# Moving an expert block's input load from GpSimd to ScalarE, in four transfers beside the result store

## What is computed

```python
def expert_block(args):                      # xb: 128 rows here; the kernel's blocks have 32
    xb, e = args
    hg, hu = jnp.split(xb @ w_gu[e], 2, axis=-1)
    return (jax.nn.silu(hg) * hu) @ w_down[e]
```

## Time and profile before

| | us |
|---|---|
| median of 3 runs (3356.11 to 3363.2) | 3362.7 |
| the profiled execution, as timed | 3372.45 |
| its span in the trace | 3370.8 |
| TensorE busy with matmuls in it | 2548.6 |
| VectorE busy | 1044.1 |
| ScalarE busy | 526.3 |
| GpSimd busy | 370.4 |

### The profile page before, as it was taken

The page is one execution under the profiler, slowest core; times in us unless marked ns, Lnnn a source line. Parts: engine busy times, 40 slices in busy tenths (PEclk is TensorE's granted clock), DMA queues, the critical chain, the costliest instruction groups (busy, mean ns, idle before and its releaser), DMA issues. The chain is left out here.

```text
span 3370.8 us, 75892 instructions
## 1 busy us (share of the span) xinstructions
PE 2548.6 (76%) x31542; PEld 1819.0 (54%) x31543; DVE 1044.1 (31%) x2767; ACT 526.3 (16%) x1257; POOL 370.4 (11%) x527
## 2 busy tenths in 40 slices
PE   8987958775998758775652897999999757667752
PEld 3456546554446446553442345989998335445531
DVE  0225322214107522211114303655653631111214
ACT  1034101101105101000001102422432000000100
POOL 0000111002000020000002001211210220000002
PEclk9988969988999869987775998987988678798976
DMA  5212059996110059999996000000000348999995
GB/s 203 81 45 113 17 194 353 366 353 225 66 75 26 15 213 366 371 375 397 391 390 242 29 25 0 1 0 0 0 0 1 134 180 318 389 380 384 367 391 194
DMA packets 110774, 646.52 MB, mean 192 GB/s; under 512 B 38290, under 2 KB 60050, under 8 KB 76900
## 3 DMA queue, kind: packets, MB, share of 16 engines
q1 hardware_dynamic: 41440, 567.30, 44.0%
q0 software_dynamic: 32896, 55.23, 5.0%
q10 hardware_dynamic: 36356, 22.86, 2.4%
HBM read 599.98 MB, written 45.09 MB: 191 GB/s over the span
## 5 line engine op out<-in xcount | busy, mean ns | idle before, releaser
L1162 PE MATMUL ps<-ring,arena 128*32 128x128 f32 x13440 | 460.1, 301 | 243.2 <-DMA ring<-in_experts 127.5
L1162 PEld LDWEIGHTS ps<-ring,arena 128*32 128x32 f32 x13440 | 422.2, 122 | 298.0 <-issue 150.0
L1171 PE MATMUL ps<-ring,arena 128*32 128x256 f32 x3360 | 263.9, 453 | 120.9 <-DMA ring<-in_experts 77.2
L1222 DVE TENSOR_TENSOR arena<-arena,ps 128x64 f32<-128x64 f32 x296 | 65.7, 222 | 713.3 <-ACT arena L1200 713.3
L1200 ACT ACTIVATE arena<-ps 128x64 f32<-128x64 f32 x296 | 66.1, 223 | 1304.3 <-PE ps L1162 1044.7
L1162 PE MATMUL ps<-arena 128*32 128x128 f32 x5504 | 189.1, 300 | 73.8 <-DMA arena<-in_experts 57.6
L1137 POOL DMA_DIRECT2D arena<-xybuf x148 | 100.3, 678 | 1277.1 <-DVE arena L1210 1235.6
L1171 PEld LDWEIGHTS ps<-ring,arena 128*32 128x32 f32 x3360 | 114.5, 126 | 231.6 <-DMA ring<-in_experts 90.8
L1162 PEld LDWEIGHTS ps<-arena 128*32 128x32 f32 x5504 | 171.6, 121 | 100.5 <-DMA arena<-in_experts 69.9
L1232 DVE COPY arena<-ps 128x256 f32<-128x256 f32 x148 | 62.9, 425 | 418.3 <-PE ps L1171 243.6
L355 PE MATMUL ps<-ring,arena 128*128 128x512 f32 x384 | 166.0, 593 | 3.1 <-PEq L192 3.1
(11 more groups left out here) (385 smaller groups left out, 3834.1 us busy)
## 6 DMA issues: line engine op xcount, KB each, us to landing
ring<-in_experts SPq DMA_DIRECT2D x165, 2048.0 KB, 38.1
arena<-in_experts SPq DMA_DIRECT2D x50, 2048.0 KB, 35.6
xt_mem<-in_experts SPq DMA_DIRECT2D x25, 2048.0 KB, 42.8
ring<-in_mixer_chunks SPq DMA_DIRECT2D x24, 2048.0 KB, 12.6
xybuf<-arena ACTq DMA_DIRECT2D x640, 32.0 KB, 11.6
arena<-xybuf POOLq DMA_DIRECT2D x160, 128.0 KB, 12.2
xybuf<-arena SPq DMA_DIRECT2D x1, 9216.0 KB, 25.6
rows<-in_ln_g POOLq DMA_DIRECT2D x6, 512.0 KB, 5.1
```

Of the source, the lines that this page charges most:

```text
L1162: ins = pe.matmul(ps[at, 2 + half, 0:P], xg[:, k, :], w_gu[half][:, k, q, :], start=(k == 0), stop=(k == NK - 1))
L1171: ins = pe.matmul(ps[at, 4, 0:W], hT[:, f, :], w_d[:, f, q * W:(q + 1) * W], start=(f == 0), stop=(f == NT - 1))
L1222: dve.tensor_tensor(hidden[:, half, :], silu_g[:, half, :], ps[:, 2 + half, HALF:P], ALU.mult)\
```

## The change

POOL only scatters. ScalarE issues the block loads, each as four transfers of 32 rows of 256 columns, two of them behind each pair of stores. It waits for the scatters, loads the first three blocks, and in block g loads block g + 3, into the buffer that block g - 1 had. Each block's four loads count up `s_loaded` by 64 instead of 16.

```diff
@@ POOL
                     for j in range(NT):
                         for n in range(2):
                             pool.indirect_dma_start(...).then_inc(s_sent, 16)
-                    pool.wait_ge(s_sent, 2 * NT * 16)
-                    fours = value(pool, slice(E + 2, E + 3), high=MAXB // AHEAD)
-                    for b in range(AHEAD):
-                        pool.dma_start(x_in[:, b, :], rows_at(b)).then_inc(s_loaded[b], 16)
-                    with pool.Fori(0, fours) as p:
-                        for b in range(AHEAD):
-                            g = AHEAD * p + b
-                            pool.wait_ge(s_xg, g + 1)
-                            pool.dma_start(x_in[:, b, :], rows_at(g + AHEAD)).then_inc(s_loaded[b], 16)
...
@@ ScalarE
+                    def rows_of_block(start, q):
+                        return xybuf[bass.ds(start, BLK), q * W:(q + 1) * W]
...
+                    def load_quarters(start, b, two):
+                        for q in two:
+                            act.dma_start(x_in[quarters[q], b, :], rows_of_block(start, q)).then_inc(s_loaded[b], 16)
...
                     fours = value(act, slice(E + 2, E + 3), high=MAXB // AHEAD)
+                    act.wait_ge(s_sent, 2 * NT * 16)
+                    for b in range(AHEAD - 1):
+                        load_quarters((b + 1) * BLK, b, range(4))
                     with act.Fori(0, fours) as p:
...
                             act.wait_ge(s_y, g + 1)
                             for half in range(2):
                                 store_quarters(g * BLK, freed, (2 * half, 2 * half + 1))
+                                load_quarters((g + AHEAD) * BLK, freed, (2 * half, 2 * half + 1))
                                 act.wait_ge(s_gu[half], g + 1)
                                 act.activation(silu_g[:, half, :], ...).then_inc(s_silu[half], 1)
...
@@ VectorE
-                            dve.wait_ge(s_loaded[after], p * 16 + 16 + 16 * (b == AHEAD - 1))
+                            dve.wait_ge(s_loaded[after], p * 64 + 64 + 64 * (b == AHEAD - 1))
```

More of the change, by code:

```diff
@@ L1089, in value @@
                 return eng.value_load(table[0:1, n], min_val=low, max_val=high)
-            def rows_at(g):
-                return xybuf[bass.ds((g + 1) * BLK, BLK), :].rearrange("r (q n) -> q r n", q=4)
             with nc.Block() as block:
@@ L1128, in _ @@
                                                     in_=x_tok[:, j, :], in_offset=None).then_inc(s_sent, 16)
-                    pool.wait_ge(s_sent, 2 * NT * 16)
-                    fours = value(pool, slice(E + 2, E + 3), high=MAXB // AHEAD)
-                    for b in range(AHEAD):
-                        pool.dma_start(x_in[:, b, :], rows_at(b)).then_inc(s_loaded[b], 16)
-                    with pool.Fori(0, fours) as p:
-                        for b in range(AHEAD):
-                            g = AHEAD * p + b
-                            pool.wait_ge(s_xg, g + 1)
-                            pool.dma_start(x_in[:, b, :], rows_at(g + AHEAD)).then_inc(s_loaded[b], 16)
-                    for b in range(AHEAD):
-                        pool.wait_ge(s_loaded[b], fours * 16 + 16)
                 @block.tensor
@@ L1182, in _ @@
                 def _(act):
+                    def rows_of_block(start, q):
+                        return xybuf[bass.ds(start, BLK), q * W:(q + 1) * W]
                     def store_quarters(start, b, two):
                         for q in two:
-                            act.dma_start(xybuf[bass.ds(start, BLK), q * W:(q + 1) * W], y_sb[quarters[q], b, :])\
-                               .then_inc(s_stored[b], 16)
+                            act.dma_start(rows_of_block(start, q), y_sb[quarters[q], b, :]).then_inc(s_stored[b], 16)
+                    def load_quarters(start, b, two):
+                        for q in two:
+                            act.dma_start(x_in[quarters[q], b, :], rows_of_block(start, q)).then_inc(s_loaded[b], 16)
                     for b in range(AHEAD - 1):
@@ L1204, in _ @@
                         act.wait_ge(s_stored[b], fours * 64 + 64)
+                    for b in range(AHEAD - 1):
+                        act.wait_ge(s_loaded[b], fours * 64 + 64)
                     act.activation(spot, eps_ln, ACT.Copy)
@@ L1213, in _ @@
                     dve.memset(spot, 0.0).then_inc(s_y, 1)
-                    dve.wait_ge(s_loaded[0], 16)
+                    dve.wait_ge(s_loaded[0], 64)
                     take_inputs(0)
```

## The result

| | before | after |
|---|---|---|
| median of 7 runs | 3363.2 us | 3391.3 us (3381.15 to 3404.6) |
| ratio | | 1.0086, 95% interval 1.0064 to 1.0108 |
| span of the profiled execution | 3370.8 us | 3392.1 us |

The change makes the kernel slower by 28 us, where 144 were forecast. The way was right. The forecast's own range, 3420 to 3600, missed it; the wider range of 3385 to 3640 holds it at its lower edge. The size was wrong by a factor of five.

What follows compares the result with a forecast made beforehand. The prediction took q10, ScalarE's queue, to bound dense stretches by its turns, one packet per weight packet, and weights to bound others. Its terms 43 + 45 + 20 + 17 + 19 = 144 us on 3362.7 gave 3507 us, range 3385 to 3640.

Steps and rivals of the forecast that it cites:

- a turn becomes shorter by 5%: Queues while weights stream: without q0's packets, turns go from 23.05 to 24.2 per us.
- rival B: Expert stages: stores' turns come 5% sooner and loads land faster, so 37 waiting copies save 15 us; 3348 us, chance 0.05.
- The shared queue: Expert stages: loads join stores on q10, 380 turns or 15.7 us a block while weights stream; terms +43, +45, +20, +17.
- my 43: First expert stage: q10 cannot follow, costing +3.3 us for each of 13 experts loaded during the stage.
- the 45 + 20: Second and third expert stages: +45 for pauses of q1 at 5.9 us each, +20 for TensorE's lag at their ends.
- The 17 for TensorE after a wait: Expert stages: slower matmuls after waiting, some 12 pauses, half of them long enough, at 2.9 us: +17 us.
- ScalarE's issuing: Expert blocks: load issues ahead of each Silu delay a block by 0.5 us, uncovered in 38 blocks: +19 us.
- The signs: Profile after: blocks about 16 us apart in stretches, dips of q1, transposes waiting for loads, loads landing in 25 to 35 us.
- The opening: Kernel start: ScalarE waits for the scatter and issues 12 loads before its table load and first Silu; cost 0.
- A: Queue q10: it takes more than a packet in a turn, or loads hide; only issuing costs, +19: 3382 us, chance 0.11.
- C: Expert stages: reserves don't help, each expert of more than one block waits for q10; 3685 us, chance 0.13.
- D: Whole kernel: nothing moves, since waits for weights cover all; 3363 us, chance 0.03.

Runs made afterwards that it cites:

- e6: As e2, but each load cut in two (eight loads of 32 rows of 512 bytes a block); 3459.55 us, 1.0267 of the kernel before.
- e10: The kernel before, POOL still loading, but in four transfers of 32 rows of 1 KB a block instead of one; 3276.41 us, ratio 0.9723.
- e2: As e1, but block g loads block g + 4 into its own buffer, a block deeper; 3334.89 us, 0.9898 of the kernel before.
- e1: The changed kernel with a block's four loads moved behind its second Silu; 3350.96 us, 0.9943 of the kernel before.
- e12: The kernel before with POOL's load as two transfers of 64 partitions instead of one; 3405.35 us, ratio 1.0104.
- e8: As e2, but the four stores too stand behind the second Silu; 3352.35 us, 0.9961 of the kernel before.
- e7: The kernel before plus a ScalarE Silu of constants behind each pair of stores, its end not waited for; 3369.03 us, ratio 1.0002.

## Why the prediction was right about the way and wrong about the size

*What bound the kernel.* Right: one packet for one packet, seen again in the changed kernel (1617 to 1616) and in e6 (2488 to 2487).

*"With q0's 5.0% out of 101.5% of the engines' time, a turn becomes shorter by 5%: 24.2 per us."* This step failed. It took the price of q0's load to be the load's own packets. In the same dense stretch 26.8 turns per us were measured (632 to 662 us), since the weights' own packets became faster: 0.570 us on average in place of 0.632. The row that could have warned was at hand: the earlier trace rows give 0.584 with few q0 packets, and 26.4 turns per us, which the forecast did not use. e10 gives the whole worth of this: the same loads by POOL without the spread shape are 2.8% faster, 93 us. The change gets that gain too: q1's packets took 1394 us in it and 1388 in e10, against 1483. My sum had no such term, and rival B, the only one with a gain, had 15 us for it.

*The shared queue.* Terms of 43 + 45 + 20 + 17 = 125 us. Between e10 and e2 the loads go from q0 to q10, with ScalarE's issues hidden: 1.75%, 59 us (in e2 they also leave later, behind the second Silu, and have 192 packets a block in place of 128; no run parts these). The smaller depth is another 15 (e2 to e1). So 74 us, in place of 125. The mechanism was as told: dips of q1 in stage one, and in the full stretches of stages two and three a block every 14 us in place of my 15.7, with 16.0 us of weights in place of 17.8. But the loss sat elsewhere. From e10 to e1 stage one grew by 305.6 - 283.5 = 22 us, half of my 43: its blocks were not 16 us apart for long, since q1 ran dry again and again and q10 drained. Stages two and three grew by 39 and 34, about the 45 + 20 that I had for both and more. That they stand at only 5 and 0 us against the kernel before is the weights' gain of 37 and 39 us in the same stages. (The three growths are 95 us together, where the whole kernel grew by 73: the stretch between stages two and three, which no change touches, took 1008.9 us in e10 and 993.4 in e1, and something between 993 and 1010 in the other runs.) The 17 for TensorE after a wait no run shows apart: its gate and up matmuls became dearer by 22 us in the three windows (649 to 671), but its whole busy time fell from 2548.6 to 2526.5 us.

*ScalarE's issuing.* Forecast +0.5 us a quiet block, 19 us; measured 1.06 us and 48 us (e1 against the change). I took 0.80 us for a pair of loads, less the 0.35 that ScalarE had to spare; but the pair costs 0.84 and 0.16 to 0.18 ahead of it, and the stores' pair went from 0.80 to 0.84, in both halves of the block, and so the second Silu is late by 1.06 and not by 0.45. And the cover that I counted on, the 8.3 us of the dense stretches, was itself removed: there most blocks take 6.5 to 9 us now, so the chain shows.

Together, relative to the kernel before: -93 + 59 + 15 + 48 = 29 us. That this meets the 28 measured is no proof: the four are the steps of one path, before to e10 to e2 to e1 to the change, and add up to the difference whatever their causes are. What they show is the size of each step at one corner of the square: along its other side, place is 31 and depth 32 us. My own terms came to 144, and the same parts measured 122; the missing -93 makes most of the error of 116. That 144 was near 122 is partly luck, since the queue's terms were 51 too large and ScalarE's 29 too small.

*The signs.* Dips of q1, waits for loads in place of waits for stores, one to one in full stretches and, there, loads landing in 25 to 35 us (33.4 from 1600 to 1660) came. Blocks 16 us apart between 560 and 750 us did not come, apart from one of 14.8 and one of 12.1, and loads landed in 9.9 us there. q10 at over twice q1's packets, which was to mean that the forecast was wrong, also appeared, 7114 to 2958, but from the stretches where q1 was dry; the sign was badly chosen. The opening came as forecast at 0: the first copy starts at 496.4 us, where it was 496.3.

*Rivals.* A and the rule of the Trainium skill on turns ("DMA: Bandwidth & Descriptors", "Queues, rings and completion order", packets of 9 to 17 descriptors) came near the time, 3382, and for a wrong reason: the records stayed at one to one, and the loads cost q10 turns. The same page's rule that the issuing engine changes only the time of the issue does not hold here: a queue of its own gave POOL's loads turns of their own (e10 against e2), which is 59 us. B's gain by shorter turns existed, by another cause and six times as large. C and D did not come.

## What to carry to other kernels

Where small transfers run beside a big stream, count packets per queue, not bytes: here a queue with work got about one packet for each large one (q10 in the changed kernel, q0 in e12), so its time is packets over turns, and moving transfers to a queue that is already full of them takes turns away. Before a transfer is priced by its own share, look whether the *others'* packets are slower beside it. On an engine that also computes, try issuing transfers behind the operation that others wait for: it gained 48 us for the loads (e1), but for stores that hid already it lost 0.6% (e8). When single steps are added up to a measured difference, see that they were measured independently: the steps of a path from one kernel to the other always add up. Here the fix was none of the change's three parts but the shape that came with it: 32-partition pieces, left on POOL.

## What was not expected of the hardware

- The packets of the weights' queue (14.6 KB on average) took 0.632 us beside POOL's one-transfer loads and 0.568 beside the same bytes in four transfers of 32 rows of 1 KB (600 to 740 us, before and e10). Over the whole kernel that is 1483 us of the engines' time against 1394 in the changed kernel.
- On POOL's queue, a load of 128 KB that spreads 4 KB rows over four groups of partitions used 144 packets and landed in 12.3 us; four quarter loads used 128 and landed in 6.6 us each; two halves used 288 and landed in 16.6 us (all from 600 to 740 us).
- A pair of ScalarE's issues took 0.80 us as stores alone and 0.84 when loads stood in between, and 0.16 to 0.18 us went between a pair of stores and a pair of loads.
- ScalarE issued two stores at 787.33 us while its own operation, begun at 786.89, ran for 1.03 us (e7), so added busy time there need not delay anything.
